# Moving loads of h and of query and gate weights ahead on the SP queue, and giving the third group of V transposes its own PSUM bank

## The reference

```
x1   = x + gate * rms_norm(mix_l @ w_out)          # end of layer 0
h    = rms_norm(x1) * (1 + scale) + shift          # start of layer 1, latent and context
z    = h @ w_in1                                   # q | k | v | g
q, k = axial_rope(q), axial_rope(k)                # latent tokens only
o    = softmax([q k_window, q k_ctx, sink]) @ [v_window, v_ctx]
out  = x1 + gate * rms_norm((o * silu(g)) @ w_out1)
```

## Time and profile before

| | us |
|---|---|
| median of 3 runs | 1451.69 |
| lowest and highest | 1446.83, 1452.19 |
| the profiled execution | 1449.23 |
| its span in the trace | 1447.0 |
| TensorE busy in the span | 1368.0 (95%) |
| VectorE busy | 859.6 (59%) |
| ScalarE busy | 735.2 (51%) |
| GpSimd busy | 522.4 (36%) |

### The profile page before, as it was taken

The page is one execution under the profiler, slowest core; times in us unless marked ns, Lnnn a source line. Parts: engine busy times, 40 slices in busy tenths (PEclk is TensorE's granted clock), DMA queues, the critical chain, the costliest instruction groups (busy, mean ns, idle before and its releaser), DMA issues. The chain is left out here.

```text
span 1447.0 us, 20170 instructions
## 1 busy us (share of the span) xinstructions
PE 1368.0 (95%) x7212; PEld 1159.1 (80%) x7212; DVE 859.6 (59%) x1243; ACT 735.2 (51%) x1151; POOL 522.4 (36%) x250
## 2 busy tenths in 40 slices
PE   5998999999999999999999989799995999998997
PEld 4777888888888888878888778688884788887686
DVE  7787868687878787861111262112213889997632
ACT  5465738382838374843212232222222899998521
POOL 0022231323131323105443324245442666667542
PEclk9999999999999999999999999999997999999999
DMA  9422131312222212373424354343336432251693
GB/s 376 163 73 101 59 109 49 114 59 99 74 84 78 94 63 80 113 280 97 137 101 130 125 181 100 105 145 106 112 116 186 153 103 88 80 153 49 198 255 110
DMA packets 93910, 177.16 MB, mean 122 GB/s; under 512 B 10368, under 2 KB 56480, under 8 KB 91552
## 3 DMA queue, kind: packets, MB, share of 16 engines
q1 hardware_dynamic: 93856, 176.44, 37.5%
HBM read 122.40 MB, written 44.06 MB: 115 GB/s over the span
## 5 line engine op out<-in xcount | busy, mean ns | idle before, releaser
L1006 PE MATMUL slab<-h_hi,w_hi 128*128 128x512 f32 x720 | 256.7, 357 | 3.1 <-DVE h_lo L363 2.3
L1007 PE MATMUL slab<-h_lo,w_hi 128*128 128x512 f32 x720 | 256.0, 356 | 0.0
L1008 PE MATMUL slab<-h_hi,w_lo 128*128 128x512 f32 x720 | 255.5, 355 | 0.0
L978 POOL TENSOR_TENSOR w_lo<-wraw,w_hi 128x1024 fp32r<-128x1024 f32 x29 | 78.8, 2716 | 304.9 <-ACT w_hi L614 304.9
L2280 POOL TENSOR_TENSOR probs<-probs,rdenom 128x2560 f32<-128x2560 f32 (+1 forms) x32 | 135.7, 4241 | 58.1 <-DVE rdenom L2239 58.1
L1006 PEld LDWEIGHTS slab<-h_hi,w_hi 128*128 128x128 f32 x720 | 136.7, 190 | 23.0 <-DVE h_lo L363 2.6
L1008 PEld LDWEIGHTS slab<-h_hi,w_lo 128*128 128x128 f32 x720 | 136.7, 190 | 19.3
L1007 PEld LDWEIGHTS slab<-h_lo,w_hi 128*128 128x128 f32 x720 | 136.8, 190 | 18.8
L1935 PE MATMUL slab<-h_hi_c,w_hi 128*128 128x512 f32 x320 | 126.5, 395 | 1.1 <-POOL w_lo L1900 1.1
L1936 PE MATMUL slab<-h_lo_c,w_hi 128*128 128x512 f32 x320 | 125.8, 393 | 0.0
L1937 PE MATMUL slab<-h_hi_c,w_lo 128*128 128x512 f32 x320 | 125.6, 392 | 0.0
(11 more groups left out here) (326 smaller groups left out, 3185.7 us busy)
## 6 DMA issues: line engine op xcount, KB each, us to landing
wraw<-in_w_in SPq DMA_DIRECT2D x32, 512.0 KB, 3.3
wm<-in_wm SPq DMA_DIRECT2D x32, 512.0 KB, 3.5
mixT<-work SPq DMA_DIRECT2D x16, 640.0 KB, 4.0
wm<-in_wm SPq DMA_DIRECT2D x8, 1024.0 KB, 17.3
mraw<-mixT SPq DMA_DIRECT2D x16, 512.0 KB, 6.1
q_parts<-qT SPq DMA_DIRECT2D x32, 256.0 KB, 4.7
oT<-o_out SPq DMA_DIRECT2D x8, 1024.0 KB, 5.3
work<-in_xT SPq DMA_DIRECT2D x8, 640.0 KB, 8.1
```

Of the source, the lines that this page charges most:

```text
L1006: nc.tensor.matmul(out, l_hi, r_hi, start=start, stop=False)
L1007: nc.tensor.matmul(out, l_hi, r_lo, start=False, stop=False)
L1008: return nc.tensor.matmul(out, l_lo, r_hi, start=False, stop=stop)
```

## The change

`first_loads` moves from step 9 of SP's loop to step 8, ahead of `load_x(8)`. The loads of slabs 4 and 5 move out of step 0 of the later loop, to before the four high and four low K stores of s = 0 (slab 4) and of s = 1 (slab 5). The third group of V transposes goes to `slab` bank 1 in round 0 and bank 5 in round 1. The first two groups use VP banks 0 and 1 in both rounds, and the waits of TensorE follow: none in round 0, and groups 0 and 1 of round 1 wait for the low parts of groups 0 and 1 of round 0.

```diff
--- before.py
+++ after.py
@@ -1321,7 +1321,7 @@
         first_loads, later_loads, proj_rest = proj_sync(sp)
 
         def body(t, s, last):
-            if last:
+            if isinstance(t, int) and t == TT - 2:
                 first_loads()
             load_x(t)
             if not (isinstance(t, int) and t >= TT - 2):
@@ -1690,9 +1690,13 @@
         t = q - CTX_TILES
         return parts[t // 4][:, :, t % 4 * P:(t % 4 + 1) * P]
 
+    def v_bank(s, g):
+
+        return VP[:, g, :] if g < 2 else slab[:, BANK[s][2], :]
+
     def v_psum(s, g, n):
 
-        return VP[:, (3 * s + g) % 2, 0:n * P].rearrange("p (t c d) -> p t c d", c=2, d=HEAD)
+        return v_bank(s, g)[:, 0:n * P].rearrange("p (t c d) -> p t c d", c=2, d=HEAD)
 
     def v_part(s, t0, n, part):
 
@@ -1739,9 +1743,9 @@
                          G[:].rearrange("p (b n) -> p b n", n=P)).then_inc(gst.sem, 16)
 
         def body(t, first, last):
-            load_slab(2 * t + 4, 0, t + 2)
-            load_slab(2 * t + 5, 1, t + 2)
             if not first:
+                load_slab(2 * t + 4, 0, t + 2)
+                load_slab(2 * t + 5, 1, t + 2)
                 store(t - 1)
 
         def rest():
@@ -1751,6 +1755,7 @@
             load_slab(2, 0, 1)
             load_slab(3, 1, 1)
             for s in range(2):
+                load_slab(4 + s, s, 2)
                 for ready, part, dst in ((rh, H, kd_hi), (rl, L, kd_lo)):
                     sp.wait_ge(ready.sem, ready.at + s + 1)
                     for c in range(2):
@@ -1941,10 +1946,10 @@
 
             pe.wait_ge(kvr.sem, kvr.at + 3 * (s + 2) + 3)
             for g, (t0, n) in enumerate(V_GROUPS):
-                if 3 * s + g >= 2:
-                    pe.wait_ge(vl.sem, vl.at + 3 * s + g - 1)
+                if s == 1 and g < 2:
+                    pe.wait_ge(vl.sem, vl.at + g + 1)
                 for i in range(n):
-                    last = nc.tensor.transpose(VP[:, (3 * s + g) % 2, i * P:(i + 1) * P], R[:, (t0 + i) * P:(t0 + i + 1) * P],
+                    last = nc.tensor.transpose(v_bank(s, g)[:, i * P:(i + 1) * P], R[:, (t0 + i) * P:(t0 + i + 1) * P],
                                                ident[:])
                 last.then_inc(vtr.sem, 1)
```

## The result

The changed kernel took 1432.85 us (median of 4 runs, 1428.28 to 1435.23), beside 1450.57 us for the kernel before (the three runs shown ahead and one more). The ratio is 0.9873, with a 95% interval of 0.9858 to 0.9887: 17.7 us less between the medians, or 1.3% by the ratio. The forecast was 1431.0.

The account below looks back on a forecast made before the run. TensorE, busy 95% of the span, was taken as the bound, so its idle time and the clock lost after it count. Terms 2.6 + 0.6 + 3.5 + 1.7 + 8.5 + 1.3 + 1.0 = 19.2 us; 1450.0 - 19 = 1431.0, range 1426 to 1435.

Parts of the forecast that it names:

- Wait before tile 8's transposes: End of layer 0's output projection: earlier first loads remove TensorE's whole wait there, 2.6 us.
- First K product: Start of the K/V products: TensorE's 0.55 us wait for the weight's low part goes, counted as 0.6 us.
- Tile 9's transposes: TensorE's 3.87 us wait before them shrinks to 0.4 us as the chain comes 7 us earlier, gain 3.5 us.
- the three subtractions 6, 7 and 8 overlap less with GpSimd: VectorE's low parts of h before tile 9: less overlap, beside 5.3 us from loads, brings the chain 7 us earlier.
- Every link of the chain but the last three is a load or waits for one: Chain to tile 9's transposes: the reason for taking the upper side, 3.5 us, of bounds 3.2 and 3.9.
- The rival that named this: Engine chain ahead of tile 9's transposes stays the bound; gap and clock fall remain, 14.0 us saved, 1436; chance 0.14.
- Clock after tile 9: With under 1 us idle before tile 9's transposes, the 5 us at clock 0.66 behind them disappear, 1.7 us.
- Third V group and clock behind it: V transposes to query product: early slabs and own bank save 8.5 us, the clock fall behind the gap 1.3 us.
- part 3 alone: Third V group's own bank without earlier slabs: TensorE would still wait for slab 4.
- part 2 alone: Earlier slabs without the own bank: TensorE would wait for one copy and one subtraction, about 1.3 us each round.
- Second round: V transposes of the second round: TensorE's 0.98 us wait goes, counted as 1.0 us.
- The rival of the K stores: Early slab 5 delays the first K stores' landing, 2 us at worst by rows; at twice that 1433; chance 0.08.

Follow-up runs that it names:

- e7: Changed kernel with VectorE's low parts of h tiles 6 to 8 made after tile 9's normalisation; 1429.51 us, 0.9847 of the kernel before.
- e10: Changed kernel with GpSimd making weight slab 1's low part only after VectorE's low part of h tile 8; 1432.42 us, 0.9862 of the kernel before.
- e8: Changed kernel with h tiles 3 and 4 loaded ahead of x tile 9 and the store of x1 tile 8; 1432.34 us, 0.9867 of before.
- e5: The changed kernel itself, run again beside the kernel before; 1430.72 us, ratio 0.9848.
- e2: Kernel before with only slabs 4 and 5 loaded ahead of the K stores; 1439.49 us, ratio 0.9914.
- e3: Kernel before with only the third V group moved to a bank of its own; 1450.89 us, ratio 0.9995.
- e6: Changed kernel with slab 5 back behind all K stores, slab 4 kept ahead; 1432.12 us, 0.9868 of the kernel before.
- e12: The changed kernel once more, run beside the kernel before; 1433.23 us, ratio 0.9869.
- e4: Kernel before with slabs 4 and 5 ahead of the K stores and the third V group's own bank, first loads unchanged; 1438.97 us, ratio 0.9915.
- e1: Kernel before with only the first loads of h and weights one step earlier; 1443.42 us, ratio 0.9941.

## Why the prediction was right

- **Wait before tile 8's transposes, 2.6 us: right**, gone. The bound that I gave for the residual held too. It took 3.38 us instead of 2.40 beside VectorE's two subtractions, which took 5.09 together:

```profile
821.24 3.38 POOL L1543 TENSOR_TENSOR x_tiles<-x_tiles,xt 128x1024 f32<-128x1024 f32 x1
```

- **First K product, 0.6 us: right.**
- **Tile 9's transposes, 3.5 us: mis-sized.** The wait shrank by 1.9 (3.87 to 1.95), since 1.95 us stayed where I had 0.4. The chain came 5.7 us earlier (39.7 us from tile 7's transposes to tile 9's became 34.0), where I had 7: 5.3 from the loads and the rest from a shorter overlap. The step that failed is "the three subtractions 6, 7 and 8 overlap less with GpSimd". Loads, copies, GpSimd's work and VectorE's moved together, so the overlap moved along, and the last subtraction took 3.29 us again. e7 and e10 show that this was the wait. "Every link of the chain but the last three is a load or waits for one" failed with it: e8 sped up two loads and gained nothing. The rival that named this (3.29 us "may again") was right about the cause and too large in its size: it left the whole gap and the fall of the clock.
- **Clock after tile 9, 1.7 us: right in the first profile** (1.00 over 851 to 856), **not in every run** (0.66 in e5). The pieces up to the V transposes come to 7.3 measured against 8.4 forecast.
- **Third V group and clock behind it, 8.5 + 1.3 = 9.8: right**, 10.3 measured. Slab 4's low part was ready here with the margin that I gave:

```profile
895.52 2.40 POOL L1905 TENSOR_TENSOR w_lo<-early,w_hi 128x1024 fp32r<-128x1024 f32 x1 [2.42 <-ACT w_hi L1791]
```

ready at 897.9, wanted at 899.7. e2 and e3 bear out "part 3 alone would leave TensorE waiting for slab 4" and "part 2 alone" waiting in each round, 0.98 us rather than 1.3.
- **Second round, 1.0: right**, 1.2.
- **The rival of the K stores** was priced at up to 2 us by rows. The wait it would lengthen went from 9.04 to 9.20 us, and e6 shows 9.16 without slab 5 behind the stores, so the effect is about 0.1 us at most. That agrees, to within this 0.1, with the rule of the Trainium skill that was weighed beside it (DMA: Bandwidth & Descriptors, Queues, rings and completion order), by which each engine consumes its ring in order.
- **The sum**: 19.2 forecast, 18.8 in the trace, 17.7 between the medians. Nothing was given back later: behind the stretch the span took 353.6 us, 354.0 before. The 1.1 us between trace and medians lies within the scatter of single runs (1446.83 to 1452.19 for the kernel before). That the trace comes so close is partly luck: in e5, the same kernel with the clock fallen after tile 9, it shows 17.2.
- **Slips in the working that changed nothing.** The bound "from the lowest run" subtracts 20.3 us, but the terms of the sum with all gaps closed come to 19.2 + 0.4 = 19.6. The 5.6 us for the landing of x is the median of the loads of h; that of x is 3.5 us, so its cover was larger than stated.

## What to carry to other kernels

A wait is put down to the instruction that came last, not to what that instruction had been queued behind; follow the queue of the engine named (here ScalarE, held 10.8 us by a weight load) before buying a buffer, since the buffer alone gave nothing that the times could show. On a strictly ordered issuing queue, look at what stands in front of a load: both loads that paid were ready long before, and stood behind a store's wait or behind the issue of sixteen stores. When a chain of several engines is moved earlier as a whole, its overlaps move with it; take no shortening of an overlap into the sum unless the order changes.

## What the runs showed of the hardware

- **Length of the wait alone does not decide whether the clock falls.** Before tile 9's transposes a wait of 2.04 us (e5) was followed by a granted clock of 0.66, and so a share of the time at 1.2 instead of 2.4 GHz, while the 5 us behind waits of 2.12 us (e6, e12) and 2.31 us (e8) were granted 1.00. In e2 it was 0.67 behind 2.81 us. Before tile 8's transposes it was 0.66 behind 2.81 us (e2) and 1.00 behind 2.83 (e4) and 3.20 (e3). All waits of more than 3.8 us in this part of the kernel (tile 9's in the kernel before, e3 and e4, the V gap in the kernel before, e1 and e3) were followed by a fall. The two profiles of the same kernel, the stretch behind the wait (e5 first, the changed kernel's first profile second, columns as in the earlier trace rows):

```profile
855.50:860.50 5.00, 4.85 (x19) 4.29 (x20) 2.50 (x3) 0.36 (x1) 0.00 (x0) 0.66 1.00 356
```

```profile
851.00:856.00 5.00, 4.99 (x26) 4.29 (x27) 2.73 (x3) 1.37 (x2) 0.00 (x0) 1.00 0.96 349
```

It costs 1.6 us when it falls. The rule of the Trainium skill that was weighed ahead of the result (TensorE: Matmul & The Clock Gate, What's actually happening), on the number of slow matmuls varying from run to run, fits this, though the page counts them at the start of a kernel and these falls are in the middle. Why one run falls and another doesn't stays open.

- **The spread of the runs comes from the first 150 us.** The same two profiles reached tile 7's transposes at 821.56 and 817.01 us. Their granted clock over the first 50 us was 0.90 and 0.97:

```profile
0.00:50.00 50.00, 34.09 (x238) 26.78 (x238) 33.80 (x72) 24.66 (x32) 0.20 (x4) 0.90 0.85 340
```

```profile
0.00:50.00 50.00, 34.11 (x264) 27.24 (x268) 37.56 (x79) 28.46 (x36) 0.20 (x4) 0.97 0.85 340
```

Over 100 to 150 us it was 0.93 and 0.97, and 1.00 in both from there to the merged part. All fourteen profiles bear this out: from 150 to 810 us TensorE was granted 1.00 and busy for 657.7 to 657.8 us in each, and tile 7's transposes came at 817.0 to 817.2 in the three with 0.97 in both early stretches and at 820.7 to 822.1 in the five with 0.90 and 0.93. These 4.5 us are more than e7 gains, so a difference of 2 us has to be read from a stretch of the trace that leaves the start out.

- **An overlap of VectorE and GpSimd can cost 2 us on one 128x1024 subtraction** (3.29 against 1.23), and it slows GpSimd too: its weight part beside that subtraction took 3.38 us, against 2.40 in e10, behind it. I had seen the long duration and not known its size to be all overlap.
